# Final norm of a decoder step: channel weights ahead of the transposes, the inverse root as a per-partition scale in the copies out of PSUM

## The reference, cut to what matters

```
D_MODEL, EPS = 1024, 1e-6

def rmsnorm(x, w):
    xf = x.astype(F32)
    y = xf * lax.rsqrt(jnp.mean(xf * xf, axis=-1, keepdims=True) + EPS)
    return (y * w.astype(F32)).astype(x.dtype)

def merge_and_ffn(x, ...):
    x = x + mix @ w_out
    h = rmsnorm(x, norm2_w)
    return x + (jax.nn.silu(h @ w_ffn_gate) * (h @ w_ffn_up)) @ w_ffn_down

    y_prompt = rmsnorm(xp, normf_w)      # (1, 512, 1024)
    y_sample = rmsnorm(xs, normf_w)      # (8, 1, 1024)
```

## Time and profile before

| what | us |
|---|---|
| median of 3 runs | 1694.37 |
| lowest and highest of them | 1694.1, 1696.58 |
| the profiled execution, its own time | 1695.87 |
| span of the profiled execution | 1694.1 |
| PE busy in the span | 1602.1 (95%) |
| DVE, ACT, POOL busy | 1007.6, 369.8, 218.4 |
| mean granted TensorE clock, share of full speed | 0.965 |

### The profile page before, as it was taken

One profiled execution on the slowest core, in us unless ns is written; L12 is line 12 of the kernel. 1 busy time (PEld: TensorE's weight loads), 2 busy tenths in 40 slices (PEclk: granted clock), 3 DMA queues, 4 the chain that ended last, 5 costly groups with the idle time before them and its releaser, 6 DMA issues. The chain is left out here.

```text
span 1694.1 us, 21865 instructions
## 1 busy us (share of the span) xinstructions
PE 1602.1 (95%) x8083; PEld 1356.9 (80%) x8083; DVE 1007.6 (59%) x1640; ACT 369.8 (22%) x817; POOL 218.4 (13%) x224
## 2 busy tenths in 40 slices
PE   6998998899999999999989999999999999999997
PEld 5886786788877787777877788888888888888885
DVE  3313886336868667686775897403786666667222
ACT  3112316422343433424232100010011000000002
POOL 1000110021322413224132000520000000000000
PEclk7999999999999999999999999978999999999997
DMA  6111114033133121331122322421322323220301
GB/s 207 50 38 51 37 51 115 12 91 100 57 104 101 57 74 57 101 88 48 50 82 75 123 79 75 138 86 55 96 75 75 99 74 99 75 92 21 129 9 51
DMA packets 153486, 131.14 MB, mean 77 GB/s; under 512 B 11411, under 2 KB 149939, under 8 KB 153411
## 3 DMA queue, kind: packets, MB, share of 16 engines
q1 hardware_dynamic: 150610, 121.93, 23.7%
q0 software_dynamic: 2816, 8.39, 1.7%
HBM read 117.26 MB, written 13.27 MB: 77 GB/s over the span
## 5 line engine op out<-in xcount | busy, mean ns | idle before, releaser
L389 PE MATMUL ps<-xn,ring 128*128 128x260 f32 (+1 forms) x2752 | 638.1, 389 | 6.0 <-ACT work L1316 1.9
L389 PEld LDWEIGHTS ps<-xn,ring 128*128 128x128 f32 (+1 forms) x2752 | 522.9, 193 | 91.9 <-ACT work L1316 2.3
L469 PE MATMUL ps<-uT,ssm_o 128*128 128x260 f32 x616 | 139.5, 383 | 0.1
L469 PEld LDWEIGHTS ps<-uT,ssm_o 128*128 128x128 f32 x616 | 117.0, 190 | 18.4 <-issue 0.4
L389 PE MATMUL ps<-ssm_o,ring 128*128 128x260 f32 x512 | 114.0, 386 | 0.0
L389 PEld LDWEIGHTS ps<-ssm_o,ring 128*128 128x128 f32 x512 | 98.3, 192 | 15.3
L469 PE MATMUL ps<-xn,ring 128*128 128x260 f32 x392 | 94.0, 383 | 0.0
L2243 POOL TENSOR_TENSOR ring<-ring 128x512 f32<-128x512 f32 x32 | 40.5, 1266 | 334.0 <-ACT ring L1422 334.0
L469 PEld LDWEIGHTS ps<-xn,ring 128*128 128x128 f32 x392 | 74.3, 190 | 11.4
L506 ACT ACTIVATE work<-ps 128x260 f32<-128x260 f32 x34 | 13.0, 381 | 321.8 <-PE ps L469 239.8
L1878 DVE TENSOR_TENSOR work<-work 128x256 f32<-128x256 f32 x24 | 18.0, 749 | 93.5 <-PE ps L1047 93.5
(11 more groups left out here) (356 smaller groups left out, 2207.9 us busy)
## 6 DMA issues: line engine op xcount, KB each, us to landing
ring<-in_w_in SPq DMA_DIRECT2D x34, 1024.0 KB, 5.3
ring<-in_w_ffn_gate SPq DMA_DIRECT2D x11, 1024.0 KB, 5.2
ring<-in_w_ffn_up SPq DMA_DIRECT2D x11, 1024.0 KB, 5.4
ring<-in_w_in SPq DMA_DIRECT2D x16, 512.0 KB, 5.3
work<-in_state_ssm SPq DMA_DIRECT2D x16, 512.0 KB, 6.5
out<-work SPq DMA_DIRECT2D x16, 512.0 KB, 4.0
ring<-in_w_ssm_br SPq DMA_DIRECT2D x8, 1024.0 KB, 7.9
ring<-in_w_ffn_down SPq DMA_DIRECT2D x8, 1024.0 KB, 5.2
```

Source lines behind the costliest of these rows:

```text
L389: mm = pe.matmul(ps[0:m, 2 * pair + h, 0:TH], lhs[k], rhs[k][:, h * TH:(h + 1) * TH], start=(k == 0), stop=(k == len(lhs) - 1))
L469: mm = pe.matmul(ps[:, bank, 0:TH], ws[k], rs[k], start=(k == 0), stop=(k == len(ws) - 1))
```

## The change

The channel weight is multiplied into `xT` in place as soon as a tile is squared (tiles 0 to 5, inside the down projection's blocks, by a new function `weigh`), or into `stage`, a buffer that is free by then (tiles 6 and 7). Additions of squares move to the same place. The transposes read the weighted, not yet normalised tiles, so PE does those of three blocks ahead of `sum_squares`; three pairs of banks hold them. `spread_norm`, `copy_norm` and the eight multiplications by `rms` go. The number of each token, `rt`, lies on the partition on which the token's row lies after the transpose, so it is applied as a per-partition scale in the copies out of PSUM: ACT copies the lower 512 channels of a block, DVE the upper 512, each with its own semaphore (`y_low`, `y_high`).

One semaphore goes elsewhere: the last instruction of GpSimd's convolution step of each group now counts `dconv_steps` instead of `dconv_done`, and those who waited for the second wait for the first at eight times the number.

```
-            sp.wait_ge(S("y_ready"), 10)
+            sp.wait_ge(S("y_low"), 5)
+            sp.wait_ge(S("y_high"), 5)
...
+            def turn_y(b, ks):
+
+                n = P if b < 4 else NB
+                for k in ks:
+                    src = xT[:, k, b * P:b * P + n] if k < 6 else stage[:, k - 6, b * P:b * P + n]
+                    mm = pe.transpose(ps[0:n, 2 * (b % 3) + k // 4, (k % 4) * P:(k % 4 + 1) * P], src, ident)
+                return mm
+
+            pe.wait_ge(S("quarter_sums"), 7 * BLOCKS)
+            pe.wait_ge(S("norm_ready"), KT + 6)
+            for b in range(3):
+                turn_y(b, range(6))
+            pe.wait_ge(S("norm_ready"), 2 * KT)
+            for b in range(3):
+                turn_y(b, (6, 7)).then_inc(S("y_turned"), 1)
             pe.wait_ge(S("squares_added"), 2 * 7 + 5)
             sum_squares(pe, NORMF, norm_sum2)
-            spread_norm(pe, NORMF)
...
+            for b in (3, 4):
+                pe.wait_ge(S("y_low"), b - 2)
+                pe.wait_ge(S("y_high"), b - 2)
+                turn_y(b, range(KT)).then_inc(S("y_turned"), 1)
...
-                        act.wait_ge(S("dconv_done"), g)
+                        act.wait_ge(S("dconv_steps"), 8 * g)
...
-            copy_norm(act, NORMF, rms)
+            act.wait_ge(S("norm_recip"), 2 * NORMF + 2)
             for b in range(5):
                 n = P if b < 4 else NB
-                dst = ytok[:, b, :] if b < 4 else ystok[0:NB, :]
+                dst = ytok[:, b, 0:512] if b < 4 else ystok[0:NB, 0:512]
                 act.wait_ge(S("y_turned"), b + 1)
-                for h in range(2):
-                    act.activation(dst[:, h * 512:(h + 1) * 512], ps[0:n, 2 * (b % 2) + h, :], ACT.Copy).then_inc(S("y_ready"), 1)
+                act.activation(dst, ps[0:n, 2 * (b % 3), :], ACT.Copy, scale=rt[0:n, b:b + 1]).then_inc(S("y_low"), 1)
...
+            def weigh(k):
+                v.wait_ge(S("norm_squared"), 2 * KT + k - 2)
+                v.tensor_scalar(xT[:, k, :], xT[:, k, :], vec[:, 2 * KT + k:2 * KT + k + 1], None,
+                                ALU.mult).then_inc(S("norm_ready"), 1)
...
+                if u:
+                    for k in (2 * u - 2, 2 * u - 1):
+                        if k:
+                            add_square(v, 2, k)
+                        weigh(k)
                 upper_sum(v, n, stage)
...
-                for k in range(max(2 * u - 2, 1), 2 * u):
-                    add_square(v, 2, k)
-            add_square(v, 2, KT - 2)
-            add_square(v, 2, KT - 1)
+            for j in range(2):
+                k = 6 + j
+                v.wait_ge(S("res_added"), KT + k + 1)
+                v.tensor_scalar(stage[:, j, :], xT[:, k, :], vec[:, 2 * KT + k:2 * KT + k + 1], None,
+                                ALU.mult).then_inc(S("norm_ready"), 1)
+            add_square(v, 2, 6)
+            add_square(v, 2, 7)
             recip_norm(v, NORMF)
-            v.wait_ge(S("norm_copied"), 2 * NORMF + 2)
-            for k in range(KT):
-                v.scalar_tensor_tensor(xn[:, k, :], xT[:, k, :], vec[:, 2 * KT + k:2 * KT + k + 1], rms,
-                                       ALU.mult, ALU.mult).then_inc(S("norm_ready"), 1)
+            v.wait_ge(S("norm_recip"), 2 * NORMF + 2)
+            for b in range(5):
+                n = P if b < 4 else NB
+                dst = ytok[:, b, 512:D] if b < 4 else ystok[0:NB, 512:D]
+                v.wait_ge(S("y_turned"), b + 1)
+                v.tensor_scalar(dst, ps[0:n, 2 * (b % 3) + 1, :], rt[0:n, b:b + 1], None,
+                                ALU.mult).then_inc(S("y_high"), 1)
```

More of the change, by code:

```diff
@@ L741, in _ @@
             for b in range(4):
-                sp.wait_ge(S("y_ready"), 2 * b + 2)
+                sp.wait_ge(S("y_low"), b + 1)
+                sp.wait_ge(S("y_high"), b + 1)
                 sp.dma_start(y_prompt[0, b * P:(b + 1) * P, :], ytok[:, b, :]).then_inc(S("stored"), 16)
-            sp.wait_ge(S("y_ready"), 10)
+            sp.wait_ge(S("y_low"), 5)
+            sp.wait_ge(S("y_high"), 5)
             sp.dma_start(y_sample[:, 0, :], ystok[0:NB, :]).then_inc(S("stored"), 16)
@@ L1402, in gate_ahead @@
                     act.wait_ge(S("ctok_done"), NG)
-                    act.wait_ge(S("dconv_done"), NG)
+                    act.wait_ge(S("dconv_steps"), 8 * NG)
                 else:
@@ L1449, in group @@
                     if i == 0:
-                        act.wait_ge(S("dconv_done"), g + 1)
+                        act.wait_ge(S("dconv_steps"), 8 * g + 8)
                     if i > 1:
@@ L2152, in _ @@
                 residual(u, 2, B_DOWN)
-                for k in range(max(2 * u - 2, 1), 2 * u):
-                    add_square(v, 2, k)
-            add_square(v, 2, KT - 2)
-            add_square(v, 2, KT - 1)
-            recip_norm(v, NORMF)
-            v.wait_ge(S("norm_copied"), 2 * NORMF + 2)
-            for k in range(KT):
-                v.scalar_tensor_tensor(xn[:, k, :], xT[:, k, :], vec[:, 2 * KT + k:2 * KT + k + 1], rms,
-                                       ALU.mult, ALU.mult).then_inc(S("norm_ready"), 1)
+            for j in range(2):
[5 more added lines that the diff above has]
+            add_square(v, 2, 7)
+            recip_norm(v, NORMF)
+            v.wait_ge(S("norm_recip"), 2 * NORMF + 2)
[5 more added lines that the diff above has]
+                                ALU.mult).then_inc(S("y_high"), 1)
         @block.gpsimd
@@ L2225, in group @@
                                 ALU.mult).then_inc(S("dconv_steps"), 1)
-                g.wait_ge(S("dconv_steps"), 7 * i + 4)
+                g.wait_ge(S("dconv_steps"), 8 * i + 4)
                 g.tensor_tensor(sc0, sc0, sc1, ALU.add).then_inc(S("dconv_steps"), 1)
                 g.tensor_tensor(sc2, sc2, sc3, ALU.add).then_inc(S("dconv_steps"), 1)
-                g.wait_ge(S("dconv_steps"), 7 * i + 6)
+                g.wait_ge(S("dconv_steps"), 8 * i + 6)
                 g.tensor_tensor(sc0, sc0, sc2, ALU.add).then_inc(S("dconv_steps"), 1)
-                g.wait_ge(S("dconv_steps"), 7 * i + 7)
-                g.tensor_tensor(xc[:, :, SEQ:T], sc0, w4[:, :, 4:5].broadcast_to((P, 4, NB)), ALU.add).then_inc(S("dconv_done"), 1)
+                g.wait_ge(S("dconv_steps"), 8 * i + 7)
+                g.tensor_tensor(xc[:, :, SEQ:T], sc0, w4[:, :, 4:5].broadcast_to((P, 4, NB)), ALU.add).then_inc(S("dconv_steps"), 1)
                 g.wait_ge(S("aux_read"), i + 1)
```

## The result

| what | before | after |
|---|---|---|
| median of the first comparison, 6 executions each, us | 1694.23 | 1685.95 |
| lowest and highest | 1693.02, 1696.58 | 1682.2, 1688.19 |
| profiled execution: time, span | 1695.87, 1694.1 | 1685.62, 1683.8 |
| last product's end to the first store's issue | 17.95 | 6.66 |
| first store's issue to the end of the span | 7.88 | 8.96 |

The span is read to 0.1 us, so the last row is good to 0.05. The ratio is 0.9948 (0.9951 from the two medians alone), with a 95% interval of 0.9935 to 0.9962. By the medians that is 8.3 us less where 11.6 were forecast, and 1685.95 lies above the range's end, 1685.0. The direction held, the size and the range did not.

A forecast was written before the change was run, and what follows sets the result against it. PE bound most of the span, store traffic its end. First store at 1675.1 plus 0.85, 5.3 and 1.25 us gave span 1682.5, 11.6 us less; with 0.3 added, median 1682.8, 0.68% less. Range 1681.6 to 1685.0.

The forecast's parts named there:

- median = span + 0.3: Whole execution: the median time lies 0.3 us above the profiled span, turning span 1682.5 into median 1682.8.
- the stores' end: Kernel's end, from first store issue: 0.85 to data, 5.3 of transfer, 1.25 after the last byte; 7.4 us in all.
- something that no row shows: Anywhere in the kernel: an unknown effect of another 1 to 3 us either way; chance 0.03.
- an end more than 8 us behind the first store: Sign at the kernel's end that would prove the prediction wrong; less than 6 us would too.
- Ahead of the sum: After the last residual: two weight multiplications (0.95 us) and two additions of squares (1.52) on DVE, ending at 1672.4.
- Transposes ahead: Before the sum of squares: 24 PE transposes end at 1671.7, beside DVE's additions, at no cost.
- Clock: PE's sum of squares at the end: stays at full clock and takes 1.18 us instead of 2.00.
- Rival 1: Clock falls during or just after the early transposes: 0.8 us more, or 2.0 if transposes slow too; chance 0.24.
- The copies: Scaled copies out of PSUM at the end: 0.68 us per 128x512 on ACT, and 0.68 taken for DVE.
- Rival 2: At the end, copies rather than stores are the bound: span end 1680.0, median 1680.3; chance 0.04.
- rival 3: At the end, both engines' copies don't run beside each other: first store 0.6 us later, 1683.4; chance 0.04.
- Down projection: Blocks 1 to 3: 2.4 us of inserted DVE work hides in 6.6 us of waiting for PE; cost 0.

The follow-up runs named there:

- The second comparison: Changed kernel run again with no edit, 5 executions, against the kernel before: 1683.25 us, ratio 0.9923 (0.9908 to 0.9938).
- The variant with late additions: Changed kernel with the additions of squares back at the end of each down block, the weight multiplications staying inside: 1688.31 us, ratio 0.9956.
- the transposes late: Changed kernel with all 24 early transposes put behind the sum of squares: 1687.99 us, ratio 0.996.
- the padding: Changed kernel with 24 one-element matmuls at the very start of PE's program, moving PE's later code against its 16 KB blocks: 1683.57 us, ratio 0.9927.
- the sum of squares first: Changed kernel with squares of tiles 6 and 7 added before their weighting, and squares summed before the last six transposes: 1682.5 us, ratio 0.9921.

## Why the prediction was wrong

The measured 1685.95 is 3.15 us above the forecast 1682.8. Two terms of the sum make nearly all of it, in about equal parts: 1.5 us are the offset between span and time, 1.3 us are the span itself (1683.8 for 1682.5), and the last 0.3 are the distance of the six executions' median from the profiled one.

**The step that failed first** is "I take median = span + 0.3". The profiled execution's own time was 1.8 us above its span, and that offset repeats: it is 1.8 in the changed kernel's trace (1685.62 against 1683.8) and 1.77 to 2.1 in 13 of 14 traces. With 1.8 in place of 0.3 the same sum gives 1684.3, and the same range reaches to 1686.5.

The median of the three executions shown, 1694.37, lies 1.5 us under the profiled execution, and that is where the 0.3 came from. It was a low draw: over all 54 executions of the kernel before in this study the median is 1695.8 (1691.49 to 1698.12), just the profiled execution's 1695.87. The first comparison drew as low, 1694.23, which is why the measured gain is 8.3 us where the spans differ by 10.3; these 2 us are luck. The twelve executions of the changed kernel have a median of 1685.55 (1681.17 to 1688.19), 10.3 us less than all 54 before. The second comparison gave 12.9 us (0.9923), and its interval holds the forecast's 0.9932; that is a draw to the other side, as the end part gives 10.2 to 11.3. The range had 0.5 us in it for scatter, and the runs shown already spread over 2.5.

**The second step that failed is the stores' end**, 1675.1 + 0.85 + 5.3 + 1.25, forecast at 7.4 us and measured at 8.96: 1.56 too little, of which an earlier first store and an earlier last product gave 0.26 back. Without a load of code it is 7.9: the bulk took exactly the 5.3 us at 400 GB/s and began 0.8 behind the issue, but 0.5 us passes until the last rows are out, a term that I left out. With a load of code among the stores it is 8.5 to 9.1, a cause that no sum of mine had. It had no rival either; it fell under "something that no row shows". The prediction's own sign for this, an end more than 8 us behind the first store, came out in the first trace and not in the other two.

What held, step by step:

- *Ahead of the sum*: it begins 4.18 us behind the last product by the forecast, 3.93 by the trace; the two weights and two additions took 2.23 us (1669.84 to 1672.07), where 2.47 were taken. To the first store: 6.83 and 6.66.
- *Transposes ahead*: hidden, done at 1671.57 (1671.7 forecast).
- *Clock*: the sum of squares took 1.19, as at 2.4 GHz. Rival 1 did not happen in any of the three traces of the changed kernel, but by a margin of 0.4 us, which nothing in the prediction had worked out; in part that was luck. Only the last sixteen transposes were at 1.2 GHz, hidden behind the stores as said. The variant with late additions shows the rival's price. The prediction held that PE's work on the transposes would keep the clock up. That is not shown: with the transposes late PE stood still for 3.93 us, and the clock held through it and most of the sum, where in the kernel before it fell 2.1 us behind the last product.
- *The copies*: ACT 0.69 for 0.68 forecast, so the 0.09 for the pointer operand holds. The Trainium skill (ScalarE: Activation LUTs, section What ACT_TABLE_LOAD costs) gives about 93 ns for it, and this trace agrees: 687 ns against 594. DVE took 0.75, more than either bound that I set:

```profile
L2183 DVE TENSOR_SCALAR ssm_o<-ps,rt 128x512 f32<-128x512 f32 x4 | 2.8, 746 | 0.8 <-PE ps L1268 0.8
L1614 ACT ACTIVATE ssm_o<-ps,rt 128x512 f32<-128x512 f32 x4 | 2.5, 687 | 1.3 <-PE ps L1268 1.0 <-DVE rt L439 0.3
```

- *The stores are the bound* once the first is out: ScalarE alone keeps up. They run at 400 GB/s. The Trainium skill (DMA: Bandwidth & Descriptors, Specifications) gives a limit of about 358 GB/s of HBM per core; the traces passed it, so the measured rate stands. Rival 2 falls, and rival 3 did not occur (copies of both engines start together at 1674.01).
- *Down projection*: cost 0. In block 2, L524 waits 1.73 for PE instead of 3.75, and L529 still 2.86, as before:

```profile
1627.48 0.41 DVE L522 TENSOR_TENSOR work<-work,ps 128x260 f32<-128x260 f32 x1
1629.63 0.43 DVE L524 TENSOR_TENSOR work<-work,ps 128x260 f32<-128x260 f32 x1 [1.73 <-PE ps L469]
...
1634.45 0.43 DVE L529 TENSOR_TENSOR work<-work,ps 128x260 f32<-128x260 f32 x1 [2.86 <-PE ps L469]
```

From the last product to the end: 14.2 us forecast, 15.62, 14.57 and 14.56 measured, 25.8 before.

**What stays open.** The first store comes 11.3 us earlier. The variants, each by itself, price the moved transposes at 1.3 us of it, the moved additions at 2.1 and the second engine for the copies at 0.5. The largest part, the spread, its copies and the eight multiplications that went, was put back in no run; it is read from the chain before, where 10.5 us lie between the reciprocal and the first store's issue, and 0.9 after the change. Which engine's code the q8 packets carry was inferred from their distance, and from the padding moving them as computed, but no row names it. Why the same kernel has the packet among its stores in one execution of three is open; in the second trace it comes at 1685.38, 2.3 us behind the end, and in the third none is recorded behind the last product. Why the clock differs near 880 us from execution to execution was not tried, nor how much of the scatter comes from there.

## What to carry to other kernels

A chain over engines can be forecast to a few tenths of a microsecond from rows of the same shapes, hand-overs included; here 6.66 against 6.83. The time that a gain is taken from, and the room for scatter in a range, need the spread of the executions: compare the profiled execution's time with its span and with the runs before choosing a base. Where a kernel ends in stores, start the first one as early as possible, and look at what else is on the DMA engines then, loads of code too. A step that runs fast on a clock about to fall has a margin, and a forecast should name it.

The best version found has the sum of squares first and the padding: 13.86 us from the last product to the end, against 14.57 for the changed kernel without a load of code. By time it can't be told from it (0.993 against 0.9923 and 0.9948), and the version without the padding had the lowest median, 1682.5.

## What the runs showed of the hardware

- A 16 KB packet on the instruction queue took 0.92 to 1.47 us where no other packet moved (31 packets from 1600 us on, in all traces), and 0.96 to 1.83 us among the stores. There the last 4 KB row was done 0.8 to 1.3 us later than in the traces without such a packet.
- The granted clock stayed at 1.00 through 3.93 us in which PE stood still in one execution, and in both traces of the kernel before fell 2.1 to 2.2 us after the last product, with PE standing still.
- A VectorE multiplication of 128x512 from PSUM by a per-partition scalar took 0.75 us, where the addition of two tensors, one of them in PSUM, takes 0.68.
